# Two transformer blocks on one core: dilated attention by pairs, unit splits and the input reordered

## What is computed

```python
outs, lses = [], []
for window, dilation in ((128, 1), (512, 4), (2048, 16)):
    o, lse = dilated_window_attention(q, k, v, window, dilation)
    ...
mix_w = jax.nn.softmax(jnp.stack(lses, axis=0), axis=0)
attn = jnp.einsum('pbsh,pbshe->bshe', mix_w, jnp.stack(outs, axis=0))
conv = short_gated_conv(bg, cg, xc, conv_w)
merged = jnp.concatenate([rms_norm_2(attn, g_attn_out), rms_norm_2(conv, g_conv_out)], axis=-1)
return merged @ w_out
```

## Time and profile before

| | us |
|---|---|
| median of 3 runs | 863.99 |
| lowest, highest | 862.1, 864.23 |
| profiled execution | 862.3 |
| its span, first to last instruction | 860.5 |
| TensorE busy | 845.9 (98%) |
| TensorE weight loads busy | 778.8 (91%) |
| VectorE busy | 541.4 (63%) |
| ScalarE busy | 394.3 (46%) |
| GpSimd busy | 4.6 (1%) |

### The profile page before, as it was taken

The page is one execution under the profiler, slowest core; times in us unless marked ns, Lnnn a source line. Parts: engine busy times, 40 slices in busy tenths (PEclk is TensorE's granted clock), DMA queues, the critical chain, the costliest instruction groups (busy, mean ns, idle before and its releaser), DMA issues.

```text
span 860.5 us, 16646 instructions
## 1 busy us (share of the span) xinstructions
PE 845.9 (98%) x7306; PEld 778.8 (91%) x7306; DVE 541.4 (63%) x597; ACT 394.3 (46%) x464; POOL 4.6 (1%) x7
## 2 busy tenths in 40 slices
PE   9999999999999999999999999999999999999997
PEld 8999889898989999999999999988898899999996
DVE  5998754545887655555558555586654765665564
ACT  7552333175377443434357343455544543444432
POOL 0000100000000000000000000000000000000000
PEclk9999999999999999999999999999999999999999
DMA  9846413321673665566544753336433465555541
GB/s 302 278 144 196 148 54 98 100 71 67 252 227 123 203 212 173 171 193 197 195 148 131 241 160 122 132 109 234 158 134 105 141 210 185 192 182 182 181 138 49
DMA packets 96747, 140.62 MB, mean 163 GB/s; under 512 B 2480, under 2 KB 79408, under 8 KB 96688
## 3 DMA queue, kind: packets, MB, share of 16 engines
q1 hardware_dynamic: 96400, 139.62, 49.3%
q10 hardware_dynamic: 288, 0.13, 0.1%
HBM read 138.69 MB, written 1.05 MB: 162 GB/s over the span
## 4 chain that ended last, share of the span: by engine, by line
PE 91%; DVE 4%; ACT 3%; issue 1%; DMA 1%; DVEq 0%; SPq 0%; ACTq 0%
PE PS L415 89%; DVE wlo L1581 2%; ACT xh L1167 1%; ACT whi L1167 1%; PE PS L520 1%; DMA xres<-in_x_dram 1%; DVE xl L1612 0%; DVE Gm L1741 0%; ACT st L1167 0%; PE PS L649 0%; PE PS L1004 0%; DVE xn L2129 0%; ACT junk L1167 0%; PE PS L1083 0%; DVE sbol L1849 0%
## 5 line engine op out<-in xcount | busy, mean ns | idle before, releaser
L1581 DVE TENSOR_TENSOR wlo<-raw,whi 128x2048 fp32r<-128x2048 f32 x124 | 283.4, 2290 | 152.4 <-ACT whi L1167 152.3
L415 PE MATMUL PS<-xh,whi 128*128 128x256 f32 x1136 | 323.5, 286 | 3.3 <-DVE wlo L1581 2.0
L415 PE MATMUL PS<-xh,wlo 128*128 128x256 f32 x1136 | 319.9, 283 | 0.0
L415 PE MATMUL PS<-xl,whi 128*128 128x256 f32 x1136 | 316.3, 283 | 0.0
L1167 ACT ACTIVATE whi<-raw 128x2048 fp32r<-128x2048 f32 (+1 forms) x130 | 240.9, 1857 | 161.3 <-PE PS L415 160.9
L415 PEld LDWEIGHTS PS<-xh,whi 128*128 128x128 f32 x1136 | 217.7, 192 | 9.8 <-issue 3.7
L415 PEld LDWEIGHTS PS<-xh,wlo 128*128 128x128 f32 x1136 | 217.8, 192 | 0.0
L415 PEld LDWEIGHTS PS<-xl,whi 128*128 128x128 f32 x1136 | 215.5, 192 | 0.9
L415 PE MATMUL PS<-whi,fh 128*128 128x512 f32 x216 | 84.4, 391 | 0.0
L415 PE MATMUL PS<-wlo,fh 128*128 128x512 f32 x216 | 84.3, 390 | 0.0
L415 PE MATMUL PS<-whi,fl 128*128 128x512 f32 x216 | 84.0, 389 | 0.0
(11 more groups left out here) (307 smaller groups left out, 1063.9 us busy)
## 6 DMA issues: line engine op xcount, KB each, us to landing
raw<-in_w_in_dram SPq DMA_DIRECT2D x32, 1024.0 KB, 5.4
raw<-in_w_up_dram SPq DMA_DIRECT2D x16, 1024.0 KB, 5.3
raw<-in_w_down_dram SPq DMA_DIRECT2D x16, 1024.0 KB, 5.0
raw<-in_w_ffn_gate_dram SPq DMA_DIRECT2D x11, 1024.0 KB, 5.4
raw<-in_w_ffn_up_dram SPq DMA_DIRECT2D x11, 1024.0 KB, 5.4
raw<-in_w_ffn_down_dram SPq DMA_DIRECT2D x11, 1024.0 KB, 5.1
raw<-in_w_kv_mem_dram SPq DMA_DIRECT2D x8, 1024.0 KB, 5.3
raw<-in_w_o_dram SPq DMA_DIRECT2D x4, 1024.0 KB, 8.1
```

The costliest lines, as they stand in the source:

```text
L415: return nc.tensor.matmul(o, l, r, start=start, stop=stop, **kw)
L1581: V.tensor_tensor(wlo[u % RING][:], raw[u % RING][:], whi[u % RING][:].bitcast(f32), ALU.subtract) \
```

## The change

- **Head.** x is loaded by column halves, and the first quarter of unit 0 stands between them. Only half of the transposes come ahead of the first products; the others stand behind the first quarter's products. Each tile column has its own place (`first`) and is waited for alone. Per quarter TensorE waits for the high half, makes the products with it, then waits for the low half. ScalarE splits unit 2 ahead of squares and root; unit 3 follows the root on ScalarE and VectorE, unit 4 the first output and so on. The norm's row is made in the middle of unit 2, the low-rank products in the middle of unit 3.
- **Recurrent stage.** The first `y_root` stands ahead of the unit's split.
- **Norms `n2`, `n3`.** ScalarE splits the second unit ahead of the second squares, VectorE ahead of the inverse. **`n4`, `n5`:** VectorE splits the first 1024 columns in two pieces between the residual adds.
- **Dilated attention.** Four pairs; logits, maxima, exponentials, transposes and values of a pair are each one step, and weights are divided before they are turned. The values come out transposed, two heads in two halves of the partitions. The attention half is then normed as the convolution half is (sum over features by ones, `ars`). The first pair's logits stand ahead of the second value unit, and the exponentials' table is loaded explicitly ahead of them.
- **End.** The first half of the last row tile is multiplied by its gains on GpSimd, scaled on ScalarE and stored from ScalarE's queue.

```diff
@@ SyncE
-            for t in range(NT):
-                sp.dma_start(xres[:, t, :], A["x"][0, t * P:(t + 1) * P, :]).then_inc(sem(f"x_loaded{t}"), 16)
+            def load_rows(c):
+                h = slice(512 * c, 512 * c + 512)
+                sp.dma_start(xres[:, :, h], A["x"][0, :, h].rearrange("(t p) n -> p t n", p=P)).then_inc(sem(f"x_loaded{c}"), 16)
+
+            load_rows(0)
...
+                        if q == 0:
+                            load_rows(1)
...
-            for i in range(2 * NT):
-                sp.wait_ge(sem("result"), i + 1)
+            for n, (t, c) in enumerate(((0, 0), (0, 1), (1, 1))):
+                sp.wait_ge(sem("result"), n + 1)
@@ TensorE, by_feature of units 0 and 1
+                    w = EARLY[u]
+                    for part in range(UNIT // w):
+                        ks = range(part * w // n, (part + 1) * w // n)
+                        if between:
+                            between(part)
+                        if (part + 1) * w < UNIT:
+                            pe.wait_ge(sem(f"part_hi{u}"), part + 1)
...
+                        for k in ks:
+                            for x_, ready in ((hi, "hi"), (lo, "xT")):
+                                if st:
+                                    pe.wait_ge(norm_sem(st, ready), nth(st, ready, k + 1))
...
+                        if (part + 1) * w < UNIT:
+                            pe.wait_ge(sem(f"part_split{u}"), part + 1)
...
@@ TensorE, first units
-            transpose_in("n1", xres, 4, lambda t, c: pe.wait_ge(sem(f"x_loaded{t}"), 16))
-            turn_over(6)
+            first_rows(0)
+            turn_over(3)
...
+            def amid_first(i):
+                if i == 0:
+                    return lambda part: first_rows(1) if part == 1 else None
+                if i == 2:
+                    return lambda f: scale_row("n1", 2)
+                if i == 3:
+                    return lambda f: lora_products()
@@ TensorE, dilated attention
+            def dilated_logits(p_):
...
+                for e in range(2):
+                    mm(PS[:, (4 + e) * 512:(4 + e) * 512 + P], q2[half(e), p_, 0:P], k2[half(e), p_, 0:P], True, True)
+                for e in range(2):
+                    last = mm(PS[:, (4 + e) * 512 + P:(4 + e) * 512 + 384], q2[half(e), p_, P:SEQ], k2[half(e), p_, :], True, True)
+                last.then_inc(sem("d_z"), 1)
+
+            def dilated_turn(p_):
+                pe.wait_ge(sem("d_w"), p_ + 1)
...
+            def dilated_values(p_):
+
+                pe.wait_ge(sem("d_q"), p_ + 1)
+                o = (6 + p_ // 2) * 512 + p_ % 2 * SEQ
+                for e in range(2):
+                    mm(PS[half(e), o:o + SEQ], v2[:, 0, head(2 * p_ + e)], dq[:, e, 0:SEQ], True, False, skip_group_check=True)
+                for e in range(2):
+                    last = mm(PS[half(e), o + P:o + SEQ], v2[:, 1, head(2 * p_ + e)], dq[:, e, SEQ:384], False, True, skip_group_check=True)
+                last.then_inc(sem("d_o"), 1)
...
+            dilated_logits(0)
+            by_token(U_V2[1], xh, xl, 4, 2, False, True)
+            for p_ in range(NPAIR):
+                if p_:
+                    dilated_logits(p_)
+                dilated_fill(2 * p_)
+                dilated_turn(p_)
+                dilated_fill(2 * p_ + 1)
+                dilated_values(p_)
             pe.wait_ge(sem("out2_evac"), 12)
-            pe.wait_ge(sem("d_z_read"), NH)
             by_token(U_VM[0], memh, meml, 0, VM_BANKS, True, False)
-            head_out(NH - 2)
-            head_out(NH - 1)
+            sum_rows(lambda j: an[:, j, :], 1, 2)
             by_token(U_VM[1], memh, meml, 2, VM_BANKS, False, False)
-
-            transpose_scaled("att", att, NPAIR, 6)
             by_token(U_VM[2], memh, meml, 4, VM_BANKS, False, False)
...
+            sum_rows(lambda j: cv[:, 1, j, :], 2, 3)
@@ ScalarE
-            for u in range(2, RING):
-                hi(u)
+            hi(3)
...
+            y_root(0)
             hi(U_G[NH - 1] + RING)
-            y_root(0)
...
                 round_T(st, g, xh, 0, range(KD), place, last_of)
+                if filler:
+                    hi(U_KM[filler - 1] - 1 + RING)
...
+            for p_ in range(NPAIR):
+                if p_:
+                    hi(FILL2[2 * p_ - 1] + RING)
+                    act.wait_ge(sem("d_T"), p_)
+                    dilated_exp(p_)
+                hi(FILL2[2 * p_] + RING)
+                act.wait_ge(sem("d_T"), p_ + 1)
+                if p_:
+                    act.wait_ge(sem("d_o"), p_)
+                A_(dq[:], PS[:, 2 * 512:4 * 512].rearrange("p (e n) -> p e n", e=2)[:, :, 0:384], ACT.Copy).then_inc(sem("d_q"), 1)
@@ VectorE
+                        if then != "fin" and (t, c) in ((0, 1), (1, 0)):
+                            lo_piece(u - 1 + RING, 512 * t, 512 * t + 512)
...
+            for p_ in range(NPAIR):
+                if p_:
+                    dilated_max(p_)
+                    lo(FILL2[2 * p_ - 1] + RING)
+                    dilated_weights(p_)
+                fill_evac(2 * p_)
+                lo(FILL2[2 * p_] + RING)
+                fill_evac(2 * p_ + 1)
             lo(FILL2[NH - 1] + RING)
@@ GpSimd, the end
+            pool.wait_ge(norm_sem("fin", "x"), nth("fin", "x", 3))
+            nc.gpsimd.tensor_tensor(xn[:, 1, 0:512], xres[:, 1, 0:512], gfin[:, 0:512], ALU.mult).then_inc(sem("gained"), 1)
```

More of the change, by code:

```diff
@@ L235, in block_kernel @@
         for n in ("T", "hi", "xT"):
-            EVENTS[n] = {n: NPAIR if n == "att" else KD for n in TURNED}
+            EVENTS[n] = {n: KD for n in TURNED}
         def norm_sem(st, what):
@@ L355, in paired, with first, itself @@
             return (1, 2, 4, 5)[f // 2], f % 2
+        def first(f):
+            return ((4, 0), (5, 0), (6, 0), (7, 0), (1, 0), (2, 0), (3, 0), (4, 1))[f]
+        def itself(f):
+            return f
         def alone(f):
@@ L1270, in _ @@
             for i, u in enumerate(U_RW):
-                if i != 1:
-                    after(u)
-                else:
+                if i == 0:
+                    hi(4)
+                elif i == 1:
                     act.wait_ge(sem("mixed"), 1)
@@ L1450, in _, with dilated_exp @@
             hi(U_V2[0] + RING)
+            nc.scalar.preload_act_table_set("exp_and_others")
+            def dilated_exp(p_):
+                act.wait_ge(sem("d_max"), p_ + 1)
+                for t, r in enumerate((slice(0, P), slice(P, 384))):
+                    for e in range(2):
+                        last = A_(dp[:, e, r], dz[:, e, r], ACT.Exp, bias=col(DMX + 4 * p_ + 2 * t + e),
+                                  accum_out=col(DL + 4 * p_ + 2 * t + e))
+                last.then_inc(sem("d_p"), 1)
+            dilated_exp(0)
             after(U_V2[1])
@@ L1563, in _ @@
                              lambda t, h: act.wait_ge(norm_sem("fin", "x"), nth("fin", "x", 2 * t + h + 1)))
+            act.wait_ge(sem("gained"), 1)
+            act.wait_ge(sem("last_scale"), 1)
+            A_(xn[:, 1, 0:512], xn[:, 1, 0:512], ACT.Copy, scale=col(NORM["fin"] + 5)).then_inc(sem("result_act"), 1)
+            act.wait_ge(sem("result_act"), 1)
+            act.dma_start(out[0, P:SEQ, 0:512], xn[:, 1, 0:512]).then_inc(sem("stored_act"), 16)
+            act.wait_ge(sem("stored_act"), 16)
         @block.vector
@@ L1633, in _ @@
                 lo_part(1, q)
+            lo(2)
             inverse("n1")
@@ L1637, in _ @@
             link(last)
-            for u in range(2, RING):
-                lo(u)
+            lo(3)
             dve.wait_ge(norm_sem("n1", "rs"), nth("n1", "rs", 1))
@@ L1913, in post, with lo_piece @@
                                                op0=ALU.mult, op1=ALU.add).then_inc(norm_sem(then, "x"), 1)
+            def lo_piece(u, a, b):
+                if a == 0:
+                    dve.wait_ge(sem("hi_done"), u + 1)
+                r = slice(a, b)
+                last = V.tensor_tensor(wlo[u % RING][:, r], raw[u % RING][:, r], whi[u % RING][:, r].bitcast(f32), ALU.subtract)
+                if b == UNIT:
+                    last.then_inc(sem("unit_split"), 1)
             def residual(base, u, b, then):
@@ L2126, in _ @@
                 dve.wait_ge(norm_sem("fin", "sd"), nth("fin", "sd", t + 1))
-                link(V.reciprocal(col(c + 4 + t), col(c + 2 + t)))
-                for h in (slice(0, 512), slice(512, D)):
+                last = V.reciprocal(col(c + 4 + t), col(c + 2 + t))
+                if t:
+                    last.then_inc(sem("last_scale"), 1)
+                    dve.wait_ge(sem("last_scale"), 1)
+                else:
+                    link(last)
+                for h in (slice(0, 512), slice(512, D))[t:]:
                     V.scalar_tensor_tensor(out=xn[:, t, h], in0=xres[:, t, h], scalar=col(c + 4 + t), in1=gfin[:, h],
```

295 lines of the change are left out of this document (125 added, 170 removed).

## The result

The changed kernel took 853.12 us (median of four executions, 850.78 to 854.01) beside 863.05 for the kernel before (four, 862.04 to 864.23): a ratio of 0.988, with a 95% interval of 0.9853 to 0.9908. A later session gave 852.0 (four, 851.85 to 854.42) beside 863.23, ratio 0.9884 (0.9864 to 0.9903). The profiled execution took 853.9 us, 852.0 of it the span, against 862.3 and 860.5 before.

What follows compares the result with a forecast made beforehand. TensorE was taken to set the end nearly everywhere, with VectorE next. Terms 5.5 + 2.5 + 1.0 + 1.1 + 0.6 - 0.1 = 10.6 us took 862.3 to 851.7; half a 1.7 us half-clock stretch made 852.5, range 849.6 to 857.

Steps and rivals of the forecast that it cites:

- Dilated stage: Dilated attention: logits and values in pairs using both array halves at once, 2.3 instead of 3.8 us per pair; net 5.5 saved.
- VectorE's cover: Dilated pair loop: VectorE finishes the scaling at T + 7.2, TensorE wants it at T + 7.5; 0.3 us to spare.
- the new wait for the `km` read: Dilated stage: first memory-value unit waits until the eighth fill has been read; 0.5 us of new wait.
- Rival 1: Dilated pair loop: VectorE's chain is 1 us late in each of three pairs, 855.5 us; chance 0.15.
- Rival 4: Dilated stage: pairs don't overlap because of another matrix order, 1.5 x 4 us given back, 858.5 us; chance 0.03.
- Norms and root: Reordered splits at the four norms save 2.5 us; root ahead of the split in the recurrent stage saves 1.0.
- Head: Kernel start: new load order and earlier splits let TensorE reach the third unit's end sooner; 1.1 us saved.
- Rival 2: Head: parameters still land at 6.2, 0.35 us saved, VectorE's backlog costs 0.5 at the reciprocal, 853.7 us; chance 0.17.
- Low-rank products: Early units: the products only move and still take 2.9 us, so nothing is gained.
- The reciprocal of `krs`: Key scaling: VectorE's reciprocal ends at about 59.9, TensorE asks at 59.8; a wait of 0.1 us.
- rival 3: Dilated stage: growing waits drop TensorE's clock to 0.50; 880 us if the whole stage is hit; chance 0.03.
- Tail: Kernel end: last results shared with GpSimd and ScalarE, both last stores start near 857.4 instead of 858.1; 0.6 us saved.

Runs made afterwards that it cites:

- 3: Changed kernel with each dilated-stage pair's matrices issued two for one half of the array, then two for the other, instead of in turn: 853.55 us.
- 4: Changed kernel with, at three dilated-stage places, all four matrices of one head (values and next logits) issued before the other head's four: 856.97 us.
- 5: Changed kernel with the four norms' split order put back as in the kernel before: 856.15 us.
- 6: Changed kernel with low-rank products in two loops, recurrent split ahead of the root, and last results on VectorE with all stores from SyncE, as before: 853.54 us.
- 10: No edit: changed kernel, and changed kernel with the krs reciprocal ahead of the key scaling, on one chip: 852.0 and 850.94 us.
- 9: Changed kernel with the krs reciprocal ahead of the key scaling, plus ScalarE's result stored from SyncE's queue like the other three: 850.67 us.
- `krs` first: Changed kernel with VectorE's maximum and reciprocal of krs moved ahead of the key-scaling loop: 849.39 us; 850.94 us in a later session.
- experiment 2: Changed kernel with the splits of the first units in the old order, one after each output: 855.86 us.

## Why the prediction was right, and where not

The forecast of 852.5 us lies between the two medians, 853.1 and 852.0. The largest terms were right; that the total was right too is owed in part to luck, since the wrong terms cancelled.

**Dilated stage, right.** 5.97 us against 5.5. A pair's 0.80 and 0.86 us are the 0.80 and 0.85 taken from the earlier trace rows. VectorE's cover, put at 0.3, was 0.40. What was over-costed is the new wait for the `km` read: it was put at 0.5, but the first memory-value matmul starts at 553.07, 0.85 us after the values at 552.22 that take 0.80, so it cost 0.05. Rival 1 did not occur. Rival 4 asked whether the order of the matrices matters; 3 shows that it doesn't at two and two, and 4 that it would have cost 1.6 us a place had the change queued each head's values and logits together.

**Norms and root, right.** 2.57 against 2.5, 0.96 against 1.0. Experiments 5 and 6 give the same sizes when they are undone, the root's with a clock stretch on top.

**Head, mis-sized: 0.33 for 1.1** (0.57 in the repeat of 10)**.** The step that failed is the end of it: "with 1.9 and 2.2 and the landing it ends near 19.3". Start and first unit were as costed (first weight product 6.64 us, unit 0 at 13.77 for a forecast of 13.7). Behind that, units 1 and 2 wait for raw weights: ScalarE starts their high halves only at 12.95 and 15.99 (12.09 and 16.61 before), after waits of 1.23 and 1.02 us for raw weights to land, and the split of unit 2 ends at 20.2. I carried over the earlier trace rows for the start and did not ask when the third unit's megabyte lands. Rival 2 named nearly this size, 0.35, but for another reason, and by its own mark it did not hold: the parameters landed at 5.1, not 6.2. The Trainium skill (DMA: Bandwidth & Descriptors, queues and rings) would have left them there if only the pieces had become shorter. The trace has them 1.1 to 1.3 us sooner than with x by rows; as half of x also moved behind the first weight quarter, no run here separates the two causes.

**Low-rank products, missed.** "Move, their 2.9 us stay" was wrong: the change also takes the two halves in turn, which the diff shows and the earlier trace rows would have priced. They take 0.97 less, shown by 6.

**The reciprocal of `krs`, the step that failed most.** The words "it reaches the point of today's 36.5 us some 1.5 us later" were wrong: VectorE reads the fourth output at 38.89, 2.42 us later. Ahead of the first output it stood idle for 1.85 us, because the extra split needs the high half of unit 3, which ScalarE starts only at 21.02, behind squares and root and a wait of 0.57 for the raw weights.

```profile
23.04 2.29 DVE L1627 TENSOR_TENSOR wlo<-raw,whi 128x2048 fp32r<-128x2048 f32 x1 [1.85 <-ACT whi L1201]
...
38.89 0.69 DVE L1684 TENSOR_TENSOR stg<-PS,rs 128x512 f32<-128x512 f32 x1
```

The pause that I counted on was there. These are the fourth and the fifth output in the kernel before:

```profile
36.47 0.68 DVE L1646 TENSOR_TENSOR stg<-PS,rs 128x512 f32<-128x512 f32 x1
...
41.70 0.69 DVE L1646 TENSOR_TENSOR stg<-PS,rs 128x512 f32<-128x512 f32 x1 [0.71 <-PE PS L415]
```

In the changed kernel the fifth is read at 43.34 without a pause, 1.64 later, and no other pause lies on the way to the reciprocal, which starts 1.63 late where the forecast had 0.8. And TensorE asked at 59.5, not 59.8, since the low-rank products were shorter. So 1.34 us of wait in place of 0.1, and behind it a stretch at half clock that costs 1.7 or 3.4 us. I named a wait here of over 0.5 as a sign of being wrong, but gave the clock no price at this place; I looked for it only in the dilated stage (rival 3), where there was none.

**Tail, wrong: 0.6 expected, nothing found.** The last store did start 0.6 us sooner, 3.56 us after the last matmul's start for 4.18. The step that failed was "0.6 saved" itself, which takes one landing time for all: behind a store issued 0.03 us before it the last one took 0.64 us longer, since the DMA engines were full (9).

**What cancelled.** By the table, the head (0.8), the tail (0.6) and the wait with its clock (4.2) fell short by 5.6 us. Against them stand the low-rank products (1.0), the surplus of the dilated stage (0.5), before's own stretch at 157.7, absent after (1.6), and units 9 to 15 (0.3): 3.4. The difference is the 2.2 us by which the profiled execution, 853.9, lies above the bare sum of 851.7. A forecast that is right by such a balance is right by less than it seems: the forecast would have missed by some 3 us had the order at `krs` been the good one.

**A better version.** `krs` first took 849.4 and 850.9 in two sessions, ratios 0.9847 (0.9828 to 0.9867) and 0.9868 (0.9852 to 0.9885) to the kernel before. Beside the changed kernel the gain is 1.1 us in the session that had both, and 2.4 over all executions; the intervals of the two kernels overlap in each session, and only all executions together set them apart. The head's missing 0.8 us are in no kernel that was run.

## What to carry to other kernels

When the engine that prepares operands is busy for 94% of a stage, lateness put in at its start arrives nearly whole at the next hand-over (here 2.4 us put in, 1.6 arrived, one pause of 0.7 between), and what only the main engine gains until there is lost; so look for the small operation in its queue (here 2 us) for which the main engine waits, and put it ahead of the bulk work for which nobody waits yet. Before you move a split forward, look when its raw weights and its high half will be there. Work for the two halves of the array has to stand close in the queue, with nothing of another shape between. At the end of a kernel look at the DMA share before you hurry the last store: where it is near 1, a sooner issue buys nothing. And a wait of a microsecond on TensorE is to be priced with the stretch at half clock that may follow, here one to three times the wait itself.

## What was not expected of the hardware

- The halves of the array overlap with two and two matrices queued as well as in turn (1.66 us for a pair's values and logits), by half with four and four of one shape (low-rank products, 2.90 us for 1.93), and not at all where two of another shape stand between (3.28 for 1.66).
- Fourteen profiled executions had fourteen stretches at half clock ahead of the last unit's end, of 3.4 or 6.8 us, each costing half of that. Two executions of the same code could differ in one or in its length. One stretch began while TensorE stood still (experiment 2).
- The last 256 KB store landed 2.04 us after its issue when the one ahead of it was 0.66 us older, and 2.68 us after when it was 0.03 us older and on the other queue; with the DMA engines 96 to 98% busy the end came at the same time.
- TensorE's first matmuls ran at half pace, 0.21 us apart, in every profiled execution: until 4.1 us in the kernel before and the changed kernel, and until 10.4 us in one execution with x by rows, where that cost over 1 us.
- GpSimd's 512-element product took 1.28 us where I had 1.1; half of its 1024 elements is not half of its time.
